# Weight sums of the down stages by accumulating transfers of GpSimd's queue

## The reference

```python
def swiglu(h, w_gate, w_up, w_down):
    return (jax.nn.silu(h @ w_gate) * (h @ w_up)) @ w_down

for i in range(DEPTH):                                # DEPTH = 2
    f = swiglu(rmsnorm(x, ffn1_pre_norm[i]), ffn1_w_gate[i], ffn1_w_up[i], ffn1_w_down[i])
    x = x + 0.5 * rmsnorm(f, ffn1_post_norm[i])
    ...                                               # mixer: GLA and SSD heads, or MLA
    f = swiglu(rmsnorm(x, ffn2_pre_norm[i]), ffn2_w_gate[i], ffn2_w_up[i], ffn2_w_down[i])
    x = x + 0.5 * rmsnorm(f, ffn2_post_norm[i])
```

## Time and profile before

| what | value |
|---|---|
| median of 3 runs | 2090.98 us (2090.63 to 2092.59) |
| profiled execution, its own time | 2093.72 us |
| span in it, first to last instruction | 2091.9 us |
| PE busy | 2078.9 us, 99% |
| DVE, ACT, POOL busy | 60%, 41%, 4% |
| granted TensorE clock, mean | 0.999 |
| DMA | 371.29 MB, mean 177 GB/s |

### The profile page before, as it was taken

One profiled execution on the slowest core, in us unless ns is written; L12 is line 12 of the kernel. 1 busy time (PEld: TensorE's weight loads), 2 busy tenths in 40 slices (PEclk: granted clock), 3 DMA queues, 4 the chain that ended last, 5 costly groups with the idle time before them and its releaser, 6 DMA issues.

```text
span 2091.9 us, 26156 instructions
## 1 busy us (share of the span) xinstructions
PE 2078.9 (99%) x10362; PEld 1746.4 (83%) x10362; DVE 1254.7 (60%) x1819; ACT 865.3 (41%) x1255; POOL 84.2 (4%) x79
## 2 busy tenths in 40 slices
PE   9999999999999999999999999999999999999998
PEld 8888888888888888988887888888897679888887
DVE  6455577476665644655457855455885547445576
ACT  5222265444555543422236532223654544222263
POOL 0000000000000000000000100000024100000000
PEclk9999999999999999999999999999999999999999
DMA  7666595222111214566568565667743124566594
GB/s 259 216 214 239 192 333 165 89 91 61 61 61 61 71 51 141 192 202 244 191 232 311 172 232 200 218 235 253 260 133 111 51 71 159 204 231 221 197 331 142
DMA packets 144412, 371.29 MB, mean 177 GB/s; under 512 B 10353, under 2 KB 10993, under 8 KB 144290
## 3 DMA queue, kind: packets, MB, share of 16 engines
q1 hardware_dynamic: 83440, 229.14, 34.4%
q10 hardware_dynamic: 60850, 140.47, 17.6%
HBM read 297.22 MB, written 71.30 MB: 176 GB/s over the span
## 4 chain that ended last, share of the span: by engine, by line
PE 90%; DVE 4%; DMA 3%; ACT 2%; issue 1%; ACTq 0%; POOL 0%; DVEq 0%; POOLq 0%; SPq 0%
PE ps L1166 18%; PE ps L1168 18%; PE ps L1167 18%; PE ps L1174 8%; PE ps L1176 8%; PE ps L1175 8%; DVE w_lo L1813 2%; DMA raw<-in_w_down 2%; PE ps L1479 1%; ACT w_hi L586 1%; DMA raw<-sums 1%; PE ps L1193 1%; PE ps L1698 1%; PE ps L1727 1%; DVE a_split L1813 1%
## 5 line engine op out<-in xcount | busy, mean ns | idle before, releaser
L1166 PE MATMUL ps<-h_hi,w_hi 128*128 128x512 f32 (+1 forms) x1832 | 680.5, 371 | 0.2
L1168 PE MATMUL ps<-h_hi,w_lo 128*128 128x512 f32 (+1 forms) x1832 | 675.1, 369 | 0.0
L1167 PE MATMUL ps<-h_lo,w_hi 128*128 128x512 f32 (+1 forms) x1832 | 674.8, 368 | 0.0
L586 ACT ACTIVATE w_hi<-raw 128x1024 fp32r<-128x1024 f32 x432 | 454.2, 1056 | 486.9 <-PE ps L1168 338.9
L1813 DVE TENSOR_TENSOR w_lo<-raw,w_hi 128x1024 fp32r<-128x1024 f32 x417 | 502.0, 1221 | 115.6 <-ACT w_hi L586 114.5
L1166 PEld LDWEIGHTS ps<-h_hi,w_hi 128*128 128x128 f32 x1832 | 345.9, 189 | 58.3 <-issue 1.8
L1168 PEld LDWEIGHTS ps<-h_hi,w_lo 128*128 128x128 f32 x1832 | 345.7, 189 | 57.2
L1167 PEld LDWEIGHTS ps<-h_lo,w_hi 128*128 128x128 f32 x1832 | 346.0, 189 | 56.0 <-issue 0.2
L1813 DVE TENSOR_TENSOR extra<-a_rows,ps 128x512 f32<-128x512 f32 x88 | 60.5, 688 | 406.1 <-PE ps L1168 382.9
L1174 PE MATMUL ps<-w_hi,a_split 128*128 128x512 f32 x616 | 241.1, 391 | 2.7 <-DVE update L1813 2.7
L1176 PE MATMUL ps<-w_hi,a_split 128*128 128x512 f32 x616 | 240.1, 390 | 0.0
(11 more groups left out here) (241 smaller groups left out, 2235.4 us busy)
## 6 DMA issues: line engine op xcount, KB each, us to landing
raw<-in_w_gate_up SPq DMA_DIRECT2D x176, 512.0 KB, 4.5
a_rows<-in_w_down ACTq DMA_DIRECT2D x44, 1024.0 KB, 9.7
sums<-a_rows ACTq DMA_DIRECT2D x44, 1024.0 KB, 7.8
raw<-sums SPq DMA_DIRECT2D x80, 512.0 KB, 5.6
raw<-in_w_down SPq DMA_DIRECT2D x60, 512.0 KB, 4.0
spilled<-extra ACTq DMA_DIRECT2D x44, 512.0 KB, 4.8
normed<-spilled ACTq DMA_DIRECT2D x44, 512.0 KB, 6.1
raw<-in_w_vg SPq DMA_DIRECT2D x16, 512.0 KB, 3.6
```

The lines of the kernel that those rows point to most:

```text
L586: return nc.scalar.activation(to, source, ACT.Copy, scale=scale)
L1166: nc.tensor.matmul(to, w_h, hi, start=first, stop=False)
L1167: nc.tensor.matmul(to, w_h, lo, start=False, stop=False)
L1168: return nc.tensor.matmul(to, w_l, hi, start=False, stop=last)
```

## The change

DVE no longer adds. GpSimd's queue gets the four additions as DMAs that accumulate: each reads a source and adds it into a destination in SBUF. The first two take their source from w_down in device memory (b12 and b22 as they are there), the third adds b11 to b22, and the fourth b22 to b21, both within SBUF. POOL waits for the load of the job, issues the first two, waits for both, issues the third, waits for it, and issues the fourth. All eleven jobs of a block stand in POOL's list between the norms of the stage before and those of the stage after. `store_job` waits for the fourth transfer. The scratch memory for the descriptors of such DMAs is raised from 1024 to 4096.

```diff
-        weight_sums = sem("weight_sums")
+        weight_sums = [sem(f"weight_sums{b}") for b in range(2)]
+        outer_sums, middle_sum = sem("outer_sums"), sem("middle_sum")
...
+            def sum_weights(f, j):                                       # POOL
+                b11, b12, b22, b21 = [job_rows[j % 2][:, n, :] for n in range(4)]
+                source = dram[f"w_down{f}"][j]
+                pool.wait_ge(job_in[j % 2], 16 * (uses(f, j, 2) + 1))
+                nc.gpsimd.dma_start(b11, source[:, 1, :], accum_op=ALU.add).then_inc(outer_sums, 16)
+                nc.gpsimd.dma_start(b12, source[:, 2, :], accum_op=ALU.add).then_inc(outer_sums, 16)
+                pool.wait_ge(outer_sums, 32 * (PAIRS * f + j + 1))
+                nc.gpsimd.dma_start(b22, b11, accum_op=ALU.add).then_inc(middle_sum, 16)
+                pool.wait_ge(middle_sum, 16 * (PAIRS * f + j + 1))
+                nc.gpsimd.dma_start(b21, b22, accum_op=ALU.add).then_inc(weight_sums[j % 2], 16)
...
+                if b in FFN_OF:
+                    for j in range(PAIRS):
+                        sum_weights(FFN_OF[b], j)
...
             def store_job(f, j):                                         # ACT
-                act.wait_ge(weight_sums, PAIRS * f + j + 1)
+                act.wait_ge(weight_sums[j % 2], 16 * (uses(f, j, 2) + 1))
                 act.dma_start(sums[f][j], job_rows[j % 2]).then_inc(job_out[j % 2], 16)
...
-                        if j == 0:                                       # DVE, ffn
-                            sum_weights(f, 0)
-                    elif tile:
-                        sum_weights(f, j)
...
-            def sum_weights(f, j):                                       # DVE
-                b11, b12, b22, b21 = [job_rows[j % 2][:, n, :] for n in range(4)]
-                dve.wait_ge(job_in[j % 2], 16 * (uses(f, j, 2) + 1))
-                signal(tt(b11, b11, b12, ALU.add))
-                after(tt(b12, b12, b22, ALU.add))
-                after(tt(b22, b11, b22, ALU.add))
-                tt(b21, b22, b21, ALU.add).then_inc(weight_sums, 1)
...
-    nc = bacc.Bacc("TRN2", ..., num_devices=1, dynamic_dma_scratch_size=1024)
+    nc = bacc.Bacc("TRN2", ..., num_devices=1, dynamic_dma_scratch_size=4096)
```

More of the change, by code:

```diff
@@ L2646 @@
     arrays = lay_out({k: np.asarray(v) for k, v in inputs.items()})
-    nc = bacc.Bacc("TRN2", target_bir_lowering=False, num_devices=1, dynamic_dma_scratch_size=1024)
+    nc = bacc.Bacc("TRN2", target_bir_lowering=False, num_devices=1, dynamic_dma_scratch_size=4096)
     dram = {k: nc.dram_tensor("in_" + k, v.shape, mybir.dt.from_np(v.dtype), kind="ExternalInput").ap() for k, v in arrays.items()}
```

## The result

| | before | after |
|---|---|---|
| median | 2091.18 us (2090.63 to 2092.59, 4 runs) | 2220.93 us (2198.61 to 2226.57, 4 runs) |
| profiled execution, its own time | 2093.72 us | 2198.61 us |
| span | 2091.9 us | 2196.8 us |
| granted TensorE clock, mean | 0.999 | 0.981 |

The ratio is 1.0597, 95% interval 1.0574 to 1.0619: the change makes the kernel 6% slower. Forecast was 2193 us, range 2089 to 2440. The profiled execution of the changed kernel is the fastest of its four; the others took 2219 to 2227 us. Lines of code have moved: 1166 to 1168 are now 1181 to 1183, 1174 to 1176 are 1189 to 1191, 1813 is 1828, 586 is 601, 598 and 602 are 613 and 617.

A forecast was written before the change was run, and what follows sets the result against it. PE was taken to bound the kernel, busy 2078.9 of 2091.9 us. Profiled 2093.7 us, plus 102 us (four blocks of 33.9 lag less 8.4 cover), less 2.7 us to the median, gave 2193 us; range 2089 to 2440.

The forecast's parts named there:

- PE bounds, and relief of DVE is worth nothing: Gate and up stages: removing 176 additions, 121 us of DVE, gains 0, at most 5.3 us, as PE never waits there.
- The chain: Each job's four transfers in three serial rounds; ACT waits for them in order, with later loads and splits behind that wait.
- A: Time from a job's load landing to its last transfer's semaphore: taken 14.6 us, bounds 9.5 to 21.9, harmless up to 12.3.
- the pace: ACT's store to store per pair in the gate and up stage: 0.57 + 9.92 + A, 25.1 us instead of 21.76.
- The rows of 5.6 and 4.5 us: Plain transfers of 512 KB and 256 KB beside other traffic, taken as prices of the first and the two later rounds.
- The lag at job 10: Lateness of ACT's last store of a block, end of gate and up stage: 11A - 126.7, 33.9 us.
- The cover: Head of the down stage: 8.4 us of lag absorbed before PE's seventh slot needs its low split; loss 25.5 us per block.
- the ring of weights: Weight splits that ACT makes six slots ahead of PE; PE's seventh down-stage slot was taken as the place that decides.
- the 102 us: Forecast loss over all four feed-forward blocks, 25.5 us each, added to the profiled execution's 2093.7 us.
- No cost of the traffic: Gate and up stages: 1 MB more per pair raises the DMA share from 0.64 to 0.78 or 0.92, which fits.
- Rival 1, hidden,: A is at most 12.3 us, so ACT's wait ends in time or the lag is covered: 2091 us; chance 0.28.
- Rival 2, dear,: Accumulation is far slower than copying, A 17.5 us or more, PE waiting mid gate and up stage; up to 2514 us; chance 0.27.

## Why the prediction was right

- *PE bounds, and relief of DVE is worth nothing.* Right: DVE is less busy in the changed kernel and no stretch is faster, and the kernel without any sums is at 1.0007.
- *The chain decides, by ACT's order.* Right. Later stores take nine tenths of the loss away and earlier loads all of it, with all the traffic in place; one round more adds 50 us per us of chain, one less all but ends it.
- *The size of A, 14.6 us.* Close. The job shown has 14.2 us, with rounds of 6.5, 4.5 and 3.2 us; the mean of jobs 2 to 10 is 15.5 us. But the load before it took 8.2 us and not 9.92; why, I did not test. The two errors stand against each other in the pace: 24.17 us measured, 25.1 forecast. The rows of 5.6 and 4.5 us, chosen because of their traffic, were a fair guide.
- *The lag at job 10.* 287.88 - 260.14 = 27.7 us, forecast 33.9: the mis-sized term. At job 1 it was 70.36 - 64.30 = 6.1 us, forecast 2A - 25.3 = 3.9; the nine pairs after it added 21.7, forecast 30.0.
- *The cover, 8.4 us.* In sum right, in place wrong. 27.7 - 8.4 = 19.3 us, and the waits per block are 19.8 on average. But PE first stops at the second slot of the down stage, for the multiplication of tile 20, and not at the seventh. I had followed the ring of weights and not `bank_free`, whose banks come free through ACT's silu and DVE's multiplication, nor `spill`, on which the second multiplication waits. Nor had I anything for the down stage after its head, where PE's wait for `update` grew from 2.7 to 14.8 us. That the sum fits is in part luck.
- *The clock.* Missing from the sum, as I had PE's busy time unchanged. PE ran at its upper level up to the waits (granted clock 1.00 from 240 to 258 us) and had 0.80 in the stretch with them. In each block 28 to 45 spacings of matmuls are slow, 25.0 us in all. That fills just what the lag was forecast too long, 4 x 6.2 = 24.8 us, so the 102 us for the profiled execution (104.9) are right in part by luck. The medians, 2221 and 2208 us, lie 28 and 15 us above 2193.
- *No cost of the traffic.* Right: 0.94 of the DMA engines' time in the kernel with earlier loads, and no loss.
- *Rival 1, hidden,* was decided against the fit of the Trainium skill ("DMA: Bandwidth & Descriptors", Anatomy of one DMA — SWDGE (gpsimd) path). It gives an estimated 2.6 us for 256 KB. A plain copy of POOL's queue within SBUF took 2.2 us at the least, so for that the trace agrees to 0.4 us. With the other traffic the plain copies' medians were 2.2 to 4.5 us, and the accumulations' 3.2 to 5.7 us. The chain of plain copies alone was 12.8 us where the fit gives 8.4, and adding made it 15.5: the fit leaves out both what a transfer loses beside traffic and what it costs to add.
- *Rival 2, dear,* wanted A of 17.5 us or more. It was 15.5, and PE does not wait from the middle of the gate and up stage on, as it does with one round more, where A is 18.9 us.

## What to carry to other kernels

Before work is moved from an engine to a queue, ask if that engine holds anybody up where the work stands; here it did not, and the best outcome was no change. Then ask for the new latency, not for the bandwidth: three rounds in series took 14 to 23 us in these kernels, and what they cost is decided by the engine that waits for them in order, and by all that stands behind its wait. If the chain is longer than its place, start it earlier. To move the wait, and to free the next load from it, was enough for the jobs that had room behind them; for the one that had none it only shifted the loss.

## What was not expected of the hardware

An accumulation from POOL's queue is dearer than a copy in three ways at once: POOL is busy 0.87 us with issuing it instead of 0.54, it lands at the least in 3.2 us instead of 2.2, and its queue takes 12.0% of the DMA engines' span instead of 5.9% for the same 46.15 MB listed, with 25344 packets instead of 14080. With a source in device memory the median is 5.5 us, with one in SBUF 3.8 (changed kernel); but the two from device memory are issued one right behind the other, so this is not the price of the source alone. DVE's low splits were not slowed by POOL's issuing: they take 1220 ns in the changed kernel and 1221 ns before, by the mean of each group.
